# Latent attention: the value products of two pairs of items in one step of TensorE, in one bank of PSUM

## The reference

```
def attend(args):
    qn, qp, b = args
    s = jnp.einsum('bqhd,bkhd->bhqk', qn, k_nope) + jnp.einsum('bqhr,bkr->bhqk', qp, k_pe)
    s = s.astype(jnp.float32) * scale
    q_idx = b * Q_BLOCK + jnp.arange(Q_BLOCK)
    s = jnp.where(key_idx[None, :] <= q_idx[:, None], s, jnp.finfo(jnp.float32).min)
    p = jax.nn.softmax(s, axis=-1).astype(dt)
    return jnp.einsum('bhqk,bkhd->bqhd', p, v)
...
return (o * jax.nn.silu(z)) @ w_out_b
```

## The kernel before

| TensorE's step | scores | turned | values before |
|---|---|---|---|
| A, n = 4q+6 | big, second of group q+1 | big, first of group q+1 | small pair 2q+1 |
| B, n = 4q+7 | small, second of group q+1 | small, first of group q+1 | none |
| C, n = 4q+8 | big, first of group q+2 | big, second of group q+1 | none |
| D, n = 4q+9 | small, first of group q+2 | small, second of group q+1 | big pair 2q+2 |

## Time and profile before

### The profile page before, as it was taken

The page is one execution under the profiler, slowest core; times in us unless marked ns, Lnnn a source line. Parts: engine busy times, 40 slices in busy tenths (PEclk is TensorE's granted clock), DMA queues, the critical chain, the costliest instruction groups (busy, mean ns, idle before and its releaser), DMA issues.

```text
span 1787.0 us, 38566 instructions
## 1 busy us (share of the span) xinstructions
PE 1750.1 (98%) x16237; PEld 1402.6 (78%) x16237; DVE 944.7 (53%) x1992; ACT 829.7 (46%) x1822; POOL 403.0 (23%) x395
## 2 busy tenths in 40 slices
PE   9999999999999999999999999999999999999998
PEld 8997776788888688977777777777777876668887
DVE  5667766424433617116556656556545267765513
ACT  5346666425434615225535535535533356655421
POOL 5650000011112433123223122122223201002221
PEclk9999999999999999999999999999999999999999
DMA  5144320143343152333222122122223310006432
GB/s 199 36 156 120 81 63 1 65 124 107 92 122 104 51 200 91 93 110 98 67 73 78 55 73 78 55 74 87 73 63 104 113 56 13 1 1 214 165 128 95
DMA packets 146004, 159.89 MB, mean 89 GB/s; under 512 B 15092, under 2 KB 123960, under 8 KB 145832
## 3 DMA queue, kind: packets, MB, share of 16 engines
q1 hardware_dynamic: 145800, 157.37, 27.8%
q0 software_dynamic: 32, 0.07, 0.0%
HBM read 110.53 MB, written 52.62 MB: 91 GB/s over the span
## 4 chain that ended last, share of the span: by engine, by line
PE 88%; ACT 4%; DVE 4%; DMA 1%; issue 1%; POOL 1%; SPq 0%; DVEq 0%; POOLq 0%; ACTq 0%
PE ps L1005 8%; PE ps L701 7%; PE ps L703 7%; PE ps L702 7%; PE ps L1007 7%; PE ps L1006 7%; PE ps L1123 4%; PE ps L816 4%; PE ps L795 3%; PE ps L895 3%; PE ps L897 3%; PE ps L896 3%; PE ps L803 3%; PE ps L1311 3%; PE ps L1334 2%; PE ps L1321 2%
## 5 line engine op out<-in xcount | busy, mean ns | idle before, releaser
L2858 POOL TENSOR_TENSOR t<-t,t 128x512 fp32r<-128x512 f32 x183 | 240.6, 1328 | 869.4 <-ACT t L1438 822.4
L1005 PE MATMUL ps<-t,t 128*128 128x512 f32 (+2 forms) x720 | 291.1, 404 | 1.7 <-POOL t L2858 1.5
L701 PE MATMUL ps<-t,t 128*128 128x256 f32 (+2 forms) x872 | 281.9, 323 | 1.9 <-ACT t L1445 1.0
L703 PE MATMUL ps<-t,t 128*128 128x256 f32 (+2 forms) x872 | 276.5, 317 | 0.0
L702 PE MATMUL ps<-t,t 128*128 128x256 f32 (+2 forms) x872 | 276.4, 317 | 0.0
L1007 PE MATMUL ps<-t,t 128*128 128x512 f32 (+2 forms) x720 | 268.0, 372 | 0.0
L1006 PE MATMUL ps<-t,t 128*128 128x512 f32 (+2 forms) x720 | 267.7, 372 | 0.0
L701 PEld LDWEIGHTS ps<-t,t 128*128 128x128 f32 x872 | 165.8, 190 | 15.5 <-issue 4.2
L702 PEld LDWEIGHTS ps<-t,t 128*128 128x128 f32 x872 | 166.0, 190 | 10.3 <-issue 0.4
L703 PEld LDWEIGHTS ps<-t,t 128*128 128x128 f32 x872 | 165.8, 190 | 10.4
L1005 PEld LDWEIGHTS ps<-t,t 128*128 128x128 f32 x720 | 135.5, 188 | 37.5 <-issue 14.1
(11 more groups left out here) (270 smaller groups left out, 3183.4 us busy)
## 6 DMA issues: line engine op xcount, KB each, us to landing
t<-in_w_in SPq DMA_DIRECT2D x53, 512.0 KB, 5.9
zgate_spill<-t SPq DMA_DIRECT2D x20, 512.0 KB, 3.0
tile_bias<-t SPq DMA_DIRECT2D x16, 576.0 KB
t<-tile_bias SPq DMA_DIRECT2D x8, 1152.0 KB, 5.9
t<-zgate_spill SPq DMA_DIRECT2D x16, 512.0 KB, 3.9
feat_spill<-t SPq DMA_DIRECT2D x13, 512.0 KB, 3.2
tile_bias<-band_bias SPq DMA_DIRECT2D x48, 128.0 KB
t<-values_and_gates SPq DMA_DIRECT2D x96, 64.0 KB
```

The lines of the kernel that those rows point to most:

```text
L701: e.matmul(dst, lh, rh, start=k == 0, stop=False)
L703: m = e.matmul(dst, ll, rh, start=False, stop=k == n - 1)
L1005: e.matmul(dst, lh, rh, start=k == 0, stop=False)
L2858: e.tensor_tensor(WLO[wslot(b)][:, o], WST[:, o], WHI[wslot(b)][:, o].bitcast(F), ALU.subtract).then_inc(w_lo.sem, w_lo.up((b, p)))
```

## The change

`latent_value(x)` becomes `latent_values(x0)`: it runs in step A alone, after the turning, and does the products of the big pair 2q and then of the small pair 2q+1 in a row, in two halves of bank 7, and after both the two transpositions of the sums. Before, the big pair's stood one step earlier (step D) and the small pair's in step A. VectorE's `latent_output` of the pairs moves from its steps 4q+6 and 4q+7 to 4q+7 and 4q+8, and both wait for the second transposition. All instructions stay the same in number and shape.

```
-            def latent_value(x):
-                n0, n1, i, c = m_pair(x)
-                pts = [m_place(n)[3] for n in (n0, n1)]
-                ob = bank_at(("ot", M_Z + x), 7, (attn_v, ("latent", x)))
-                if i > 3:
-                    w.wait_ge(*prob_lo[M_Z + n1, 0])
-                w.wait_ge(*prob_hi[M_Z + n1, int(i > 3)])
+            def latent_values(x0):
+
+                two = (x0, x0 + 1)
+                ob = bank_at(("ot", M_Z + x0), 7, *[(attn_v, ("latent", x)) for x in two])
+                where["ot", M_Z + x0 + 1] = 7
                 w.wait_ge(*lat_a["vn", NT - 1])
-                for k in range(i + 1):
-                    for s in range(2):
-                        e.matmul(ob[64 * s:64 * s + 64, 0:128], VN[:, k, 128 * c + 64 * s:128 * c + 64 * s + 64], pts[s][:, tile128(k)], start=k == 0, stop=k == i)
-                w.wait_ge(*lat_a["sums", x])
-                m = e.transpose(ob[:, 128:256], RSB[x % 2][:, :], ident)
-                m.then_inc(value_mm.sem, value_mm.up(("latent", x)))
+                for x in two:
+                    n0, n1, i, c = m_pair(x)
+                    pts = [m_place(n)[3] for n in (n0, n1)]
+                    if i > 3:
+                        w.wait_ge(*prob_lo[M_Z + n1, 0])
+                    w.wait_ge(*prob_hi[M_Z + n1, int(i > 3)])
+                    o = 256 * (x % 2)
+                    for k in range(i + 1):
+                        for s in range(2):
+                            e.matmul(ob[64 * s:64 * s + 64, o:o + 128], VN[:, k, 128 * c + 64 * s:128 * c + 64 * s + 64], pts[s][:, tile128(k)], start=k == 0, stop=k == i)
+                for x in two:
+                    o = 256 * (x % 2) + 128
+                    w.wait_ge(*lat_a["sums", x])
+                    m = e.transpose(ob[:, o:o + 128], RSB[x % 2][:, :], ident)
+                    m.then_inc(value_mm.sem, value_mm.up(("latent", x)))
...
-                if m_valued(n) is not None:
-                    latent_value(m_valued(n))
+                if n > 5 and n % 4 == 2:
+                    latent_values((n - 6) // 2)
...
-                o, ob = ZT[:, c, tile128(i)], psum(("ot", M_Z + x))
+                o, ob = ZT[:, c, tile128(i)], psum(("ot", M_Z + x))[:, 256 * (x % 2):256 * (x % 2) + 256]
                 w.wait_ge(*lat_v["gate", c])
-                w.wait_ge(*value_mm["latent", x])
+                w.wait_ge(*value_mm["latent", x + 1 - x % 2])
...
-            for n in range(64 + 4):
-                if n and m_valued(n - 1) is not None:
-                    latent_output(m_valued(n - 1))
+            for n in range(64 + 5):
+                if n > 6 and n % 4 in (3, 0):
+                    latent_output((n - 7) // 4 * 2 + (n - 7) % 4)
```

## The result

The changed kernel takes 1800.12 us (median of 4 runs, 1799.31 to 1801.96) against 1788.97 us (4 runs, 1787.21 to 1790.25): the ratio is 1.0063, 95% interval 1.0047 to 1.0079, 11.2 us slower. The profiled execution took 1800.79 us with a span of 1798.1 us, 11.1 us over the span before.

What follows compares the result with a forecast made beforehand. TensorE, busy 98% of the span, was taken to bound the kernel. Rounds 12.1 us more, beginning 2.4 less, end 1.4 more: 11.1 us on 1789.95 gave 1801.1 us, own range 1795 to 1807, widened to 1794.5 to 1809.

Steps and rivals of the forecast that it cites:

- What the change removes: TensorE, each group: one visit of value products less, 0.15 + 0.17 = 0.32 us, 5.1 us in 16 groups.
- The link from the sums to the copy: Step A: VectorE's copy waits for the transposition behind all 36 records, 2.12 us of products, 0.37 us until seen.
- The rounds: From one step A turning to the next: four groups 40.06 us, 14 rounds 139.7 us against 127.5 before, 12.1 more.
- The signs: Profile after: products in runs of 36, step A copy some 3 us behind its turning, longer TensorE waits for exponentials and copies.
- The beginning: First step A has no step D products ahead: its turning starts at 1468.16 instead of 1470.59, 2.4 us less.
- The end: From the last step A turning to the first product needing the last output: 13.9 us instead of 12.5, 1.4 more.
- The sum: Whole program: 12.1 - 2.4 + 1.4 = 11.1 us more, the saved change of mode included.
- Hidden waits: Rival: step A's copy is not held, so the stage only loses 5.1 us: 1784.9 us; 5 in 100.
- The hold showing at bank 5 alone: Rival: TensorE loses only step B's 0.4 us per group, exponentials catch up: 1791.2 us; 6 in 100.
- More than one link more: Rival: late copy also delays small items' exponentials and sums, 0.5 us more a round: 1808 us; 11 in 100.

Runs made afterwards that it cites:

- The last experiment: Kernel after plus third buffer and ScalarE's exponential ahead of the small item's copy; against it, each pair's sums transposed right behind its own products: 1789.8 us.
- hold alone: Kernel before, products in place, but step A's two copies of the big item also wait for the small pair's transposed sums: 1800.2 us, ratio 1.0064.
- the third buffer: Kernel after the change, but the turned big items go round three buffers instead of two: 1789.9 us, ratio 1.0006 to the kernel before.
- the sums in between: Kernel after the change, two buffers, but each pair's sums transposed right behind its own products: 1797.1 us, ratio 1.0047 to the kernel before.
- the products first: Kernel after the change, two buffers, but TensorE's step A does both pairs' products and sums before turning the big item: 1790.4 us, ratio 1.0011.
- the third buffer with the new order: Kernel after with three buffers for turned big items and, in ScalarE's step A, the exponential ahead of the small item's copy: 1784.1 us, ratio 0.9974.
- the three made from it: Kernel before with, singly: a third buffer (1788.6 us), the longer wait of step A's copies (1800.2), ScalarE's exponential ahead of the small item's copy (1787.7).

## Why the prediction was right

The time (1801.1 foretold, 1800.1 measured), its sign and the place of the loss came out. Step by step:

- **What the change removes.** 5.1 us for one visit less in each of 16 groups, inside the sum. The last experiment has 4.8 us by its trace and 5.4 us by its ratio. The Trainium skill says that a change of tiling mode drains TensorE ("TensorEngine Tiling (Array Packing)", Tiling Modes, Key Properties). The traces agree, with 0.30 us for a visit; as a forecast of the time by itself the rule would have had the wrong sign. The 0.17 us that the prediction read in front of such changes is no proof by itself: the scores' loads show 0.24 us where no mode changes, as at 1506.53 in the kernel after.
- **The link from the sums to the copy.** Foretold 2.12 us of products and 0.37 us until VectorE sees them; measured 2.12 (1508.96 to 1511.08) and 0.44 us. That the held copy is the cause is shown from both sides, by taking it away (1789.9 us) and by adding a shorter hold alone (1800.2 us).
- **The rounds.** Turnings of step A in the timeline of weight loads of the kernel after, four rounds of 6, 5, 8 and 7 tiles:

```profile
1477.88 0.64 PEld L1321 LDWEIGHTS ps<-t,t 128*128 128x128 f32 x6 [0.56 <-ACT t L1964]
...
1487.67 0.53 PEld L1321 LDWEIGHTS ps<-t,t 128*128 128x128 f32 x5 [0.47 <-ACT t L1964]
...
1497.73 0.86 PEld L1321 LDWEIGHTS ps<-t,t 128*128 128x128 f32 x8 [0.89 <-ACT t L1964]
```

  With 1508.05 and 1517.78 from above: 9.79, 10.06, 10.32 and 9.73 us, against 9.66, 10.17, 10.41 and 9.82 foretold; 39.90 against 40.06. The 14 rounds took 139.3 us (1468.14 to 1607.43), 139.7 foretold. That each round came so close is in part luck, since two terms erred in opposite directions. With 7 tiles it was 3.47 us to the first copy (3.34 foretold), 2.87 to the turning of step C (2.84), 0.77 to the second copy (1.03) and 2.62 to the next turning (2.61). The 1.03 us were the durations of reciprocal, two outputs and mask added up, but these begin only 0.08 to 0.31 us behind each other (1514.37, 1514.45, 1514.76, 1514.96, and the copy at 1515.16).
- **The signs.** The products stand in runs of 36. The copy of step A waits for the transposed sums 15 times, up to 3.4 us, and the turnings wait 22.6 us for the exponentials (15 to 25 foretold) and 16.5 us for the copies (15 to 20).
- **The beginning.** The first such turning came at 1468.14; 1468.16 was foretold.
- **The end** was the one stretch whose sum was mis-sized: 13.9 us foretold, 14.8 measured (1607.43 to 1622.22). Timeline of the kernel after, and of what stood there before:

```profile
1620.28 1.28 POOL L3116 TENSOR_TENSOR t<-t,t 128x512 fp32r<-128x512 f32 x1 [20.08 <-ACT t L1930]
1620.75 1.35 DVE L2779 TENSOR_TENSOR t<-t,t 128x512 fp32r<-128x512 f32 x1 [0.70 <-ACT t L1930]
...
1622.22 0.19 PEld L1360 LDWEIGHTS ps<-t,t 128*128 128x128 f32 x1 [1.67 <-issue]
```

```profile
1609.82 0.69 DVE L2772 TENSOR_TENSOR t<-t,t 128x512 fp32r<-128x512 f32 x1 [0.70 <-ACT t L1923]
```

  The last subtraction on VectorE took 1.35 us instead of 0.69; most of the missing 0.9 us is that. From the last transposed sums (1618.45) to this load it was 3.77 us, 3.1 foretold.
- **The sum.** 139.3 less 127.5 in the rounds, 2.45 less at the beginning, 2.27 more at the end: 11.6 us up to 1622.22, which stood at 1610.63. The span grew by 11.1 us, so 0.5 us were won back elsewhere, which I have not followed.
- **The rivals.** Hidden waits (1784.9 us): its condition, the copy 0.64 us behind its turning, is what the third buffer makes (0.70 us), and even then it needs ScalarE's order too (1784.1 us). The hold showing at bank 5 alone: it was 0.7 us in each step B, but the exponentials did not catch up. More than one link more: no such link shows in the rounds, which came out 0.16 us shorter in four than foretold.
- **What was right by less than it seemed.** The prediction let either the maximum or ScalarE's small copy start the exponential of step A, and with two buffers both come at nearly the same time (at 7 tiles the small copy was over at 1513.12, the maximum at 1513.21). It had no sentence on what ScalarE's order costs once the copy is free. Of my later expectations, those for the third buffer, the hold alone and the sums in between missed their ranges by it, as told above; those for the products first and for the third buffer with the new order missed for other reasons. ScalarE's order is a second hold of 5.8 us behind the first.

## What to carry to other kernels

When work moves past another instruction of the same queue, look for the buffers that it frees: their next writers now wait for it, and what stood beside the chain becomes a link of it. Taking one hold away (10.2 us here) can uncover another, over half as long (5.8 us), in a second in-order queue. Its sign is an engine that idles for the operand of one instruction while the operand of the instruction behind it is ready. A saving on the leading engine (here 0.3 us a group) is worth having only if the change leaves the cover of its waits in place.

## What the runs showed of the hardware that was not expected

The last subtraction of VectorE, 128x512 from two tiles in SBUF, took 0.69 us in the kernel before and the three made from it, where GpSimd's like subtraction (1.28 us) had ended before it. It took 1.35 us in all seven kernels that raise both last outputs together, where GpSimd's had begun 0.47 or 0.48 us earlier and was still running (in the kernel after, 1620.28 to 1621.56). VectorE's ended at 1622.10, 0.54 us behind it. The Trainium skill has a rule for it ("SBUF — State Buffer", SBUF: two separate sides): VectorE with two inputs in SBUF and GpSimd share one pair of ports, and the later one is blocked until the earlier is through. The traces agree in kind; a full 0.69 us after the end of GpSimd's row they do not show, and no run changes this overlap alone, so that the ports are the cause is not shown here.
